# Modulation vectors on VectorE: 512 columns at a time, four blocks a TensorE turn

## The chip, the cores and the metric

The kernel runs on one core of one Trainium2 chip. The metric is the device time of one execution in microseconds (us), the median of several runs. TensorE is called PE, VectorE DVE, ScalarE ACT, GpSimd POOL and SyncE SP, as in the profile. TensorE's clock has two levels, 2.4 GHz and 1.2 GHz; the profile gives the granted share of the higher one.

## The reference, cut to what matters

Two transformer blocks on 512 tokens of width 1024, all in float32: a first block (retention heads, attention, a gated merge, a feed-forward of width 4096) and a second of two layers (with 256 context tokens beside the 512 in the first layer). Each block scales and shifts its activations by vectors that come from a conditioning vector:

```python
def ada_params(cond, w, b):
    m = jax.nn.silu(cond) @ w + b          # cond: [1024], w: [1024, 6144]
    return jnp.split(m, 6, axis=-1)        # shift, scale, gate (twice)

def modulate_2(h, shift, scale):
    return h * (1 + scale) + shift
```

The second block takes two such vectors per layer (one for the tokens, one for the context) from the same weights. In all that is three weight matrices of 1024 x 6144, or 3 x 48 blocks of 128 output columns. The first 16 blocks are needed before the first weight product and are computed ahead of it; this is not touched. The other 128 blocks, numbered a = 0 to 127, are computed beside the rest: a = 0 to 31 with one vector (first block), 32 to 79 and 80 to 127 with two (the layers of the second block).

## The kernel before, in words

Every large weight product is done in units of 256 weight columns (`gemm`, L543 to L545). A unit with 8 row tiles of 128 (KT = 8) has 48 matmuls of 512 columns, one with 4 row tiles has 24; with context, half as many again of 256 columns. The float32 weights are split in two parts: SP loads `raw`, ACT copies it to `w_hi` (`hi`, L1066 or L1074), DVE subtracts to get `w_lo` (`lo`, L1600), and PE multiplies hi by hi, hi by lo and lo by hi. Buffers alternate between two units: `hi(n+1)` waits until unit n-1 is done, so `hi` and `lo` of the next unit must fit beside unit n on PE. PE's unit n+2 also waits until ACT has taken the results of unit n out of PSUM (`psum_free`). In the second half of a feed-forward ACT takes them to `y_t` (L1342) and DVE adds them to X (`residual`, L1859); in the first half ACT takes `r_t` (L1325), DVE squares it (L1843), ACT and DVE split it (L1847).

The order of each engine's instructions is written out by hand, with loops over heads and over feed-forward blocks; the tables at the top of the file say after which unit a piece of modulation work is placed. Before the change one block a of 128 columns goes this way:

- POOL loads all 8 row tiles of the block into `ada_raw` (L2204), multiplies by the conditioning vector with a broadcast (L2213), and adds the 8 row tiles in three halvings (L2215, L2217, L2219), once per vector; then it raises `ada_sum`. Before block a it waits until PE has done step a-2.
- PE sums over the partitions: one product with a column of ones for each vector (`ada_mm_step`, L671), placed after a unit. It waits for `ada_sum` and for `ada_evac`, that is until DVE has taken the result of the block before. Each product appears as two records in the profile. The result lies in one PSUM column per vector.
- DVE takes it out and adds the bias (`ada_out` L1643, `ada_outs` L1653), and raises `ada_evac`.

In each of the four retention heads there are eight such steps (L664 to L730). The order on DVE there is: `lo(n+1)`; for heads 1 to 3 `z_f32(h-1)`, a reciprocal and eight scaled products that end the head before (L1659, L1662, L1666); a take; `lo(n+2)`; `z_low`; a take; and on. On PE it is: `gemm(n)`, a step, `gemm(n+1)`, a step, the four short units of the z product (L543 with z_hi), and on. `rotate` (L1680 to L1686) stands on DVE between the `lo` of the second and of the third of these short units.

Of the kernel before, what the change touches and what calls it, by code (L numbers as in the profile page):

```python
# [58 lines left out]
ADA = {"gate_a": [1, 1, 0, 1], "ret_out": [0, 1, 0, 0], "att0": [1, 1, 1, 1, 0, 1, 1, 1, 0], "att1": [1, 1, 1, 1, 0, 1, 1, 1, 0],  # L59
       "gate_b": [1, 1, 0, 1], "att_out": [0, 1, 0, 0], "w_o": [1, 1, 1, 1],  # L60
       "ff_head": [1, 1], "ff_body": [1, 0, 0, 1, 0, 1, 0, 1, 0, 1, 0, 1], "ff_tail": [1, 0, 0, 0, 1, 0, 0, 0, 0, 0],
       "w_in_0": [1] * 9, "w_out_0": [1] * 4, "ff_head_0": [1, 1], "ff_body_0": [1, 1, 0, 1, 1, 1, 1, 1, 0, 1, 1, 1],
       "ff_tail_0": [1, 0, 1, 0, 1, 0, 0, 0, 0, 0]}
# [37 lines left out]
def ada_starts():  # L101

    start, a = {}, 32
    for name in ADA:
        start[name] = a
        a += sum(ADA[name]) * (3 if "body" in name else 1)
    return start, a
# [18 lines left out]
def build(nc, d, out):  # L126
    FU, RESULTS, WITH_CTX = unit_plan()
    ADA0, ADA_END = ada_starts()
    assert ADA0["w_in_0"] == 80 and ADA_END == 128, (ADA0, ADA_END)
# [7 lines left out]

    def ada_first(name, k, i=0):
        return ADA0[name] + sum(ADA[name][:k]) + (i * sum(ADA[name]) if "body" in name else 0)
# [6 lines left out]
    with ctx:  # L146
# [4 lines left out]
        def sem(name):  # L151
# [3 lines left out]
        o = 16512  # L155
# [29 lines left out]
        ada_raw = [at(f"ada_raw{i}", [P, KT, P], F32, o + 4096 * i) for i in range(2)]  # L185
        ada_prod = at("ada_prod", [P, KT, P], F32, o + 8192)
        ada_acc = at("ada_acc", [P, 2, 2, P], F32, o + 12288)
        o += 14336
# [31 lines left out]
                at("ada0_2", [P, KT, 512], F32, F1 + 40960), at("ada0_3", [P, KT, 512], F32, 16512 + 32768)]  # L220
# [320 lines left out]
        def _(pe):  # L541
# [121 lines left out]
            ada_par = [0]  # L663

            def ada_mm_step(a, vecs=1, bank_=C1):

                pe.wait_ge(ada_sum, a + 1)
                if not (isinstance(a, int) and a == 0):
                    pe.wait_ge(ada_evac, a)
# [5 lines left out]
            def ada_steps(name, k, i=0):  # L675

                for j in range(ADA[name][k]):
                    ada_mm_step(ada_first(name, k, i) + j, 2, X1 if name.endswith("_0") else C1)

            def ret_head(h, n, with_out, first=False):  # L680
                gemm(n, 0, hs_hi, hs_lo, ready=(hs_ready, lambda k: k + 1) if first else None)
                ada_mm_step(8 * h)
                gemm(n + 1, 1, hs_hi, hs_lo)
                ada_mm_step(8 * h + 1)
# [19 lines left out]
                ada_mm_step(8 * h + 2)  # L704
                ada_mm_step(8 * h + 3)
# [12 lines left out]
                ada_mm_step(8 * h + 4)  # L718
                ada_mm_step(8 * h + 5)
# [11 lines left out]
                ada_mm_step(8 * h + 7)  # L731
# [4 lines left out]
            for j in range(4):  # L736
                gemm(FU["gate_a"] + j, j % 2, hs_hi, hs_lo)
                ada_steps("gate_a", j)
            for j in range(4):
                if j == 0:  # L740
                    pe.wait_ge(zlo_done, 4)
                gemm(FU["ret_out"] + j, j % 2, z_hi, z_lo, 4)
                ada_steps("ret_out", j)
# [33 lines left out]
            for p_ in range(2):  # L777
                n = FU["att0"] + 9 * p_
                for hh in range(2):
                    for g in range(GROUPS):  # L780
                        gemm(n + 6 * hh + g, (n + 6 * hh + g) % 2, hs_hi, hs_lo)
                        ada_steps(f"att{p_}", 6 * hh + g)
                    if hh == 0:
                        for g in range(GROUPS):
                            gemm(n + 3 + g, (n + 3 + g) % 2, hs_hi, hs_lo, tokens=tile_tok)
                            ada_steps(f"att{p_}", 3 + g)
# [14 lines left out]
            for j in range(4):  # L801
                gemm(FU["gate_b"] + j, (FU["gate_b"] + j) % 2, hs_hi, hs_lo)
                ada_steps("gate_b", j)
            for j in range(4):
# [3 lines left out]
                ada_steps("att_out", j)  # L808
            for j in range(4):
                gemm(FU["w_o"] + j, j % 2, m_hi, m_lo, ready=(mlo_done, lambda k: k + 1) if j == 0 else None)  # L810
                ada_steps("w_o", j)
            norm_sums()

            def feed_forward(n0, sec, nr, mf, ready, cready, suffix):
# [4 lines left out]
                def ada_(name, k, i=0):  # L819
                    if suffix is not None:  # L820
                        ada_steps(name + suffix, k, i)
# [68 lines left out]
            for l in range(2):  # L890
# [7 lines left out]
                for u in range(9):  # L898
# [5 lines left out]
                    if wc:  # L904
                        ada_steps("w_in_0", u)
                pe.wait_ge(psum_free, R(n + 9))
                if wc:
                    pe.wait_ge(ada_evac, ada_first("w_out_0", 0))
# [121 lines left out]
                for j in range(4):  # L1030
                    gemm(n + 9 + j, (n + 9 + j) % 2, hs_hi, hs_lo, cact=(hc_hi, hc_lo) if wc else None)
                    if wc:
                        ada_steps("w_out_0", j)
# [521 lines left out]
        def _(dve):  # L1555
# [84 lines left out]
            def ada_out(a):  # L1640

                dve.wait_ge(ada_mm, a + 1)
                dve.tensor_tensor(mod1[:, bass.ds(16 + a, 1)], C1[:, 0:1], vec1[:, bass.ds(24 + a, 1)],  # L1643
                                  ALU.add).then_inc(ada_evac, 1)

            def ada_outs(name, k, i=0):

                l, bank_ = (1, X1) if name.endswith("_0") else (0, C1)
                for j in range(ADA[name][k]):
                    a = ada_first(name, k, i) + j  # L1650
                    dve.wait_ge(ada_mm, a + 1)
                    j_ = a - (80 if l else 32)
                    dve.tensor_scalar(mod2[l][:, :, bass.ds(j_, 1)], bank_[:, 0:2].rearrange("p (v o) -> p v o", o=1),  # L1653
                                      vec2[:, l, bass.ds(j_, 1)], None, ALU.add).then_inc(ada_evac, 1)
# [40 lines left out]
            def ret_head(h, n, with_out):  # L1695
# [3 lines left out]
                ada_out(8 * h)  # L1699
# [3 lines left out]
                ada_out(8 * h + 1)  # L1703
# [630 lines left out]
```

## Time and profile before

| | |
|---|---|
| median of three runs | 3314.33 us (3310.28 to 3318.7) |
| the profiled execution | 3322.18 us, its span 3320.5 us |
| mean granted clock of TensorE | 0.955 |
| busy: PE, DVE, ACT, POOL | 3055.3, 1714.8, 1181.4, 1347.8 us |
| stages, from PE's timeline | start to about 92 us, heads to 554, gates and attention to 1040, feed-forward of the first block to 1431, second block's first layer to about 2549, second layer to 3290 |

Times in rows are microseconds from the start of the span. A busy PE means that its stream of matmuls goes on; two matmuls of 512 columns start 0.23 us apart though each is shown as 0.39 us long, since they overlap. What costs time is where the start of a matmul comes later than that. POOL is busy in the table's sense only with its arithmetic; issuing a transfer takes it under a microsecond.

### The profile page before, as it was taken

How to read it: one execution, taken by the hardware profiler on the slowest of the kernel's cores; microseconds unless marked ns; L12 is line 12 of the kernel's file. 1: busy time of each engine (PE TensorE's matmuls, PEld its weight loads, DVE VectorE, ACT ScalarE, POOL GpSimd, SP SyncE). 2: the span in 40 equal slices, each digit the busy share in tenths (PEclk: the TensorE clock that was granted, in tenths of full speed). 3: DMA queues.
4: the chain of work that ended last, by engine and by line, in shares of the span. 5: the costliest groups of instructions: out<-in, count | busy, mean ns of one | idle time of the engine just before them, and what ended most of it. 6: DMA issues, size and time to landing. Idle time of an engine off the chain costs nothing.

```text
span 3320.5 us, 42497 instructions
## 1 busy us (share of the span) xinstructions
PE 3055.3 (92%) x16079; PEld 2564.3 (77%) x16079; DVE 1714.8 (52%) x1792; ACT 1181.4 (36%) x1683; POOL 1347.8 (41%) x1044
## 2 busy tenths in 40 slices
PE   5799999999988999989988989999999988989998
PEld 3677777788776788859787768787887968868886
DVE  4563454533355776651286357555554338444444
ACT  2232333223333333342255343232324326433443
POOL 2455346774556777716500147777770000000000
PEclk7899999999999999999997899999999999999999
DMA  8333332453433344322310112222322230013331
GB/s 268 115 107 100 113 118 89 138 151 101 125 100 104 102 127 133 120 65 89 99 36 1 32 58 89 90 89 83 96 83 77 69 94 3 26 57 102 95 101 64
DMA packets 260466, 307.50 MB, mean 93 GB/s; under 512 B 23467, under 2 KB 231739, under 8 KB 260316
## 3 DMA queue, kind: packets, MB, share of 16 engines
q1 hardware_dynamic: 234716, 224.43, 21.7%
q0 software_dynamic: 19456, 72.00, 7.2%
q10 hardware_dynamic: 6144, 8.91, 0.9%
q8 instruction: 112, 1.84, 0.2%
q14 instruction: 38, 0.31, 0.0%
HBM read 294.05 MB, written 11.27 MB: 92 GB/s over the span
## 4 chain that ended last, share of the span: by engine, by line
POOLq 32%; PE 32%; issue 26%; DVE 5%; DVEq 1%; POOL 1%; SPq 1%; ACT 1%; DMA 0%; ACTq 0%
POOLq L2214 12%; POOLq L2216 9%; PE psum L543 9%; PE psum L544 8%; PE psum L545 8%; POOLq L2218 6%; POOLq L2222 4%; POOL ada_raw L2204 1%; PE psum L877 1%; PE psum L715 1%; DVE w_lo L1600 1%; PE psum L887 1%; SPq L434 1%; PE psum L621 1%; PE psum L700 1%
## 5 line engine op out<-in xcount | busy, mean ns | idle before, releaser
L2213 POOL TENSOR_TENSOR ada_prod<-ada_raw,csil 128x1024 f32<-128x1024 f32 x224 | 458.6, 2047 | 728.7 <-PE psum L671 708.4
L543 PE MATMUL psum<-hs_hi,w_hi 128*128 128x512 f32 x1632 | 655.3, 402 | 61.3 <-DVE hs_lo L1592 35.5
L1600 DVE TENSOR_TENSOR w_lo<-raw,w_hi 128x2048 fp32r<-128x2048 f32 (+1 forms) x244 | 535.7, 2196 | 292.5 <-ACT w_hi L1066 226.1
L545 PE MATMUL psum<-hs_lo,w_hi 128*128 128x512 f32 x1632 | 644.4, 395 | 0.0
L544 PE MATMUL psum<-hs_hi,w_lo 128*128 128x512 f32 x1632 | 644.3, 395 | 0.0
L2215 POOL TENSOR_TENSOR ada_prod<-ada_prod 128x512 f32<-128x512 f32 x224 | 365.0, 1630 | 193.4 <-issue 179.6
L543 PEld LDWEIGHTS psum<-hs_hi,w_hi 128*128 128x128 f32 x1632 | 312.5, 192 | 132.1 <-issue 44.1
L545 PEld LDWEIGHTS psum<-hs_lo,w_hi 128*128 128x128 f32 x1632 | 311.8, 191 | 67.8
L544 PEld LDWEIGHTS psum<-hs_hi,w_lo 128*128 128x128 f32 x1632 | 313.0, 192 | 63.2
L543 PE MATMUL psum<-mid_hi,w_hi 128*128 128x512 f32 x768 | 303.4, 395 | 4.0 <-DVE w_lo L1600 3.9
L545 PE MATMUL psum<-mid_lo,w_hi 128*128 128x512 f32 x768 | 300.1, 391 | 0.0
L544 PE MATMUL psum<-mid_hi,w_lo 128*128 128x512 f32 x768 | 299.6, 390 | 0.0
L1859 DVE TENSOR_TENSOR X<-X,y_t 128x512 f32<-128x512 f32 x208 | 197.1, 957 | 171.9 <-ACT y_t L1342 171.9
L1843 DVE TENSOR_TENSOR r_t<-r_t 128x512 f32<-128x512 f32 x112 | 119.3, 1067 | 314.5 <-ACT r_t L1325 314.4
L1342 ACT ACTIVATE y_t<-psum,mod 128x512 f32<-128x512 f32 x208 | 143.1, 690 | 338.3 <-PE psum L545 320.0
L2217 POOL TENSOR_TENSOR ada_prod<-ada_prod 128x256 f32<-128x256 f32 x224 | 247.0, 1103 | 31.9
L1325 ACT ACTIVATE r_t<-psum 128x512 f32<-128x512 f32 x112 | 67.0, 599 | 455.8 <-PE psum L545 455.7
L543 PE MATMUL psum<-w_hi,hs_hi 128*128 128x256 f32 x704 | 200.3, 285 | 0.0
L544 PE MATMUL psum<-w_hi,hs_lo 128*128 128x256 f32 x704 | 199.2, 283 | 0.0
L545 PE MATMUL psum<-w_lo,hs_hi 128*128 128x256 f32 x704 | 199.2, 283 | 0.0
L1074 ACT CAST w_hi<-raw 128x2048 fp32r<-128x2048 f32 (+1 forms) x138 | 190.6, 1381 | 0.0
L1066 ACT CAST w_hi<-raw 128x2048 fp32r<-128x2048 f32 (+1 forms) x106 | 174.3, 1645 | 14.8 <-issue 8.9
(332 smaller groups left out, 5668.0 us busy)
## 6 DMA issues: line engine op xcount, KB each, us to landing
raw<-in_w_in SPq DMA_DIRECT2D x56, 1024.0 KB, 5.1
ada_raw<-in_ada_w POOLq DMA_DIRECT2D x96, 512.0 KB, 4.7
raw<-in_w_ff SPq DMA_DIRECT2D x48, 1024.0 KB, 5.5
raw<-in_w_ff SPq DMA_DIRECT2D x96, 512.0 KB, 3.5
ada_raw<-in_w_ada POOLq DMA_DIRECT2D x32, 512.0 KB, 4.7
raw<-in_w_in SPq DMA_DIRECT2D x24, 512.0 KB, 5.2
ada<-in_w_ada SPq DMA_DIRECT2D x4, 2048.0 KB, 24.1
raw<-in_w_ret_out SPq DMA_DIRECT2D x16, 512.0 KB, 3.4
```

The costliest lines, as they stand in the source:

```text
L543: pe.matmul(dst, lhi, rhi, start=start, stop=False)
L544: pe.matmul(dst, llo, rhi, start=False, stop=False)
L545: return pe.matmul(dst, lhi, rlo, start=False, stop=stop)
L1074: act.copy(w_hi[n0_ % 2][:, 0:kt], raw[n0_ % 2][:, 0:kt]).then_inc(hi_done, 1)
L1600: dve.tensor_tensor(w_lo[par][:, 0:kt], raw[par][:, 0:kt], w_hi[par][:, 0:kt].bitcast(F32), ALU.subtract).then_inc(lo_done, 1)
L1859: dve.tensor_tensor(X[:, q, :], X[:, q, :], y_t[r_][:], ALU.add).then_inc(y_free, 1)
L2213: pool.tensor_tensor(ada_prod[:], ada_raw[par][:], bass.AP(c_.tensor, c_.offset, [*c_.ap, [0, P]]), ALU.mult)
L2214: pool.drain()
L2215: pool.tensor_tensor(ada_prod[:, 0:4], ada_prod[:, 0:4], ada_prod[:, 4:8], ALU.add)
L2216: pool.drain()
L2217: pool.tensor_tensor(ada_prod[:, 0:2], ada_prod[:, 0:2], ada_prod[:, 2:4], ALU.add)
L2218: pool.drain()
```

## The change

PE and DVE are given other modulation work, and POOL only issues the loads. The 128 blocks become 32 groups g of 512 columns (four blocks). A load brings two row tiles of 512 columns (the same 512 KB as before), so a group has four loads; the work on one load is a slot s = 0 to 127.

- DVE does a slot with one operation per row tile and vector: the first of a group multiplies (`tensor_scalar`), the others multiply and add to `ada_acc` (`scalar_tensor_tensor`), all on 128 x 512, with a drain between the row tiles. That is two operations for a slot of the first 32 and four for the others. It raises `ada_sum` after each slot.
- PE does a turn per group: it waits for `ada_sum` >= 4g+4 and `ada_evac` >= g, and does four blocks for each vector one behind the other.
- DVE takes four columns per vector at once (`ada_take1`, `ada_take2`).
- POOL waits before load s until slot s-2 is done.
- The tables say where slots, turns and takes stand. In a head slots 0 and 1 stand behind `lo(n+4)`, 2 to 4 behind `lo(n+5)`, 5 to 7 behind `lo(n+6)`.
- `ada_prod` goes, the SBUF offsets move, and the scratch for POOL's transfers is halved (`dynamic_dma_scratch_size=8192`).

```diff
+ADA_SLOTS = {"gate_a": [1] * 4, "att0": [1] * 8 + [0], "att1": [1] * 8 + [0], "gate_b": [1] * 4,
+             "ff_body": [1, 1, 1, 0, 1, 0] * 2, "w_in_0": [2] * 8 + [0], "w_out_0": [1] * 4,
+             "ff_body_0": [1, 1, 1, 0, 1, 0] * 2, "ff_tail_0": [1] * 4 + [0] * 6}
+
+ADA_TURNS = {"gate_a": {0: 7}, "ret_out": {0: 8}, "att0": {4: 9}, "att1": {0: 10, 4: 11}, "gate_b": {0: 12}, "att_out": {0: 13},
+             "ff_body": {5: 14, 11: 15}, "w_in_0": {2: 20, 4: 21, 6: 22, 8: 23}, "ff_head_0": {1: 24},
+             "ff_body_0": {5: 25, 11: 26}, "ff_tail_0": {4: 31}}
+
+ADA_TAKES = {"gate_a": {0: 6, 2: 7}, "ret_out": {2: 8}, "att0": {6: 9}, "att1": {2: 10, 6: 11}, "gate_b": {2: 12},
+             "ff_body": {0: 13, 6: 14}, "ff_tail": {0: 19}, "w_in_0": {3: 20, 5: 21, 7: 22},
+             "ff_body_0": {0: 24, 6: 25}, "ff_tail_0": {0: 30, 5: 31}}
...
+            def ada_turn(g, par, vecs=1, bank_=C1):
+
+                pe.wait_ge(ada_sum, 4 * g + 4)
+                if not (isinstance(g, int) and g == 0):
+                    pe.wait_ge(ada_evac, g)
                 for v in range(vecs):
-                    mm = pe.matmul(bank_[:, v:v + 1], ada_acc[:, ada_par[0], v, :], ones_c[:, 0:1], start=True, stop=True)
-                ada_par[0] ^= 1
+                    for b in range(4):
+                        mm = pe.matmul(bank_[:, 4 * v + b:4 * v + b + 1], ada_acc[par][:, v, b * P:(b + 1) * P], ones_c[:, 0:1],
+                                       start=True, stop=True)
                 mm.then_inc(ada_mm, 1)
...
             def ret_head(h, n, with_out, first=False):
                 gemm(n, 0, hs_hi, hs_lo, ready=(hs_ready, lambda k: k + 1) if first else None)
-                ada_mm_step(8 * h)
+                if with_out:
+                    ada_turn(2 * h - 1, 1)
                 gemm(n + 1, 1, hs_hi, hs_lo)
-                ada_mm_step(8 * h + 1)
...
-                ada_mm_step(8 * h + 6)
                 gemm(n + 5, 1, hs_hi, hs_lo)
+                ada_turn(2 * h, 0)
                 pe.wait_ge(gsq_done, h + 1)
...
+            def ada_slot(s, i=None, two=True):
+
+                par, kp = s % 2, s % 4
+                acc = ada_acc[s // 4 % 2]
+                if kp:
+                    dve.drain()
+                dve.wait_ge(ada_in[par], 16 * (s // 2 + 1) if i is None else 64 * i + 16 * (s // 2 + 1))
+                for kk in range(2):
+                    k = 2 * kp + kk
+                    if kk:
+                        dve.drain()
+                    for v in range(2 if two else 1):
+                        c_ = csil2[:, v, k:k + 1] if two else csil[:, k:k + 1]
+                        if k == 0:
+                            last = dve.tensor_scalar(acc[:, v, :], ada_raw[par][:, kk, :], c_, None, ALU.mult)
+                        else:
+                            last = dve.scalar_tensor_tensor(out=acc[:, v, :], in0=ada_raw[par][:, kk, :], scalar=c_,
+                                                            in1=acc[:, v, :], op0=ALU.mult, op1=ALU.add)
+                last.then_inc(ada_sum, 1)
...
                 lo(n + 1, 1)
                 if with_out:
                     z_f32(h - 1)
-                ada_out(8 * h)
+                    ada_take1(2 * h - 2)
                 lo(n + 2, 0, 4 if with_out else KT)
                 if with_out:
                     z_low(h - 1)
-                ada_out(8 * h + 1)
+                    ada_take1(2 * h - 1)
...
-                ada_out(8 * h + 2)
-                ada_out(8 * h + 3)
                 lo(n + 4, 0)
-                ada_out(8 * h + 4)
-                ada_out(8 * h + 5)
+                for s in range(2):
+                    ada_slot(s, h, False)
                 lo(n + 5, 1)
+                for s in range(2, 5):
+                    ada_slot(s, h, False)
                 dve.wait_ge(mu_done, h + 1)
                 dve.tensor_tensor(ro[:], ro[:], bc(X1[:], 4), ALU.subtract).then_inc(d_sub, 1)
-                ada_out(8 * h + 6)
                 lo(n + 6, 0)
-                ada_out(8 * h + 7)
+                for s in range(5, 8):
+                    ada_slot(s, h, False)
...
+            def load_ada(w, c, kp, par):
+                pool.dma_start(ada_raw[par][:], w[:, 2 * kp:2 * kp + 2, bass.ds(c, 512)]).then_inc(ada_in[par], 16)
```

In the units of a feed-forward and of the attention a slot stands behind `lo` of the next unit and ahead of `residual` or of the squares.

## Rows read from the trace of the kernel before

**Rows 1.** The page's busy table, whole span.
```profile
PE 3055.3 (92%) x16079; PEld 2564.3 (77%) x16079; DVE 1714.8 (52%) x1792; ACT 1181.4 (36%) x1683; POOL 1347.8 (41%) x1044
```
**Rows 2.** PE's timeline (start, duration in us): steps between products of weights.
```profile
565.60 0.50 PE L671 MATMUL psum<-ones_c,ada_acc 128*128 128x1 f32 x4
565.96 0.49 PE L543 MATMUL psum<-hs_hi,w_hi 128*128 128x512 f32 x1
...
207.03 0.28 PE L671 MATMUL psum<-ones_c,ada_acc 128*128 128x1 f32 x2
207.17 0.48 PE L543 MATMUL psum<-hs_hi,w_hi 128*128 128x512 f32 x1
```
**Rows 3.** PE's timeline: stops in the feed-forward with context.
```profile
2140.94 0.28 PE L545 MATMUL psum<-midc_lo,w_hi 128*128 128x256 f32 x1
2146.30 1.01 PE L671 MATMUL psum<-ones_c,ada_acc 128*128 128x1 f32 x4 [5.08 <-POOL ada_acc L2219]
2150.19 0.79 PE L543 MATMUL psum<-hs_hi,w_hi 128*128 128x512 f32 x1 [2.88 <-issue]
...
2443.97 1.01 PE L671 MATMUL psum<-ones_c,ada_acc 128*128 128x1 f32 x4 [5.16 <-POOL ada_acc L2219]
```
**Rows 4.** PE's timeline: stops that DVE ends, the idle time in brackets.
```profile
144.60 0.35 PE L671 MATMUL psum<-ones_c,ada_acc 128*128 128x1 f32 x2 [0.76 <-DVE mod L1643]
...
220.72 0.49 PE L543 MATMUL psum<-z_hi,w_hi 128*128 128x512 f32 x1 [2.29 <-DVE z_lo L1672]
...
235.67 0.49 PE L543 MATMUL psum<-z_hi,w_hi 128*128 128x512 f32 x1 [2.15 <-DVE w_lo L1600]
...
581.46 0.80 PE L543 MATMUL psum<-hs_hi,w_hi 128*128 128x512 f32 x1 [3.97 <-DVE w_lo L1600]
...
991.32 0.79 PE L543 MATMUL psum<-m_hi,w_hi 128*128 128x512 f32 x1 [5.53 <-DVE w_lo L1600]
```
**Rows 5.** Groups by line (busy us, mean ns): 1075 to 1430 us, then 2960 to 3290.
```profile
L1859 DVE TENSOR_TENSOR X<-X,y_t 128x512 f32<-128x512 f32 x62 | 76.5, 1251 | 27.9 <-ACT y_t L1342 27.9
...
L1859 DVE TENSOR_TENSOR X<-X,y_t 128x512 f32<-128x512 f32 x63 | 43.4, 692 | 62.2 <-ACT y_t L1342 62.2
L1600 DVE TENSOR_TENSOR w_lo<-raw,w_hi 128x1024 fp32r<-128x1024 f32 x32 | 39.2, 1225 | 8.0 <-ACT w_hi L1074 6.0 <-ACT w_hi L1066 2.0
...
L1074 ACT CAST w_hi<-raw 128x1024 fp32r<-128x1024 f32 x24 | 25.0, 1043 | 0.0
```
**Rows 6.** Stretches: length, then busy PE, PEld, DVE, ACT, POOL; granted clock.
```profile
2150.00:2153.00 3.00, 2.81 (x7) 2.24 (x8) 2.06 (x1) 0.00 (x0) 1.15 (x1) 0.50 0.25 85
221.00:226.00 5.00, 5.00 (x16) 3.91 (x16) 5.00 (x3) 0.56 (x1) 4.48 (x4) 0.66 0.33 101
1075.00:1430.00 355.00, 349.21 (x1564) 287.74 (x1563) 248.29 (x194) 136.53 (x172) 265.10 (x198) 1.00 0.40 121
```
**Rows 7.** PE's timeline: first and last product of two feed-forwards.
```profile
1061.43 0.77 PE L543 MATMUL psum<-hs_hi,w_hi 128*128 128x512 f32 x1 [13.35 <-DVE hs_lo L1592]
...
1431.44 0.39 PE L545 MATMUL psum<-mid_lo,w_hi 128*128 128x512 f32 x1
...
2939.69 0.77 PE L543 MATMUL psum<-hs_hi,w_hi 128*128 128x512 f32 x1 [8.74 <-DVE hs_lo L1592]
...
3290.50 0.39 PE L545 MATMUL psum<-mid_lo,w_hi 128*128 128x512 f32 x1
```
**Rows 8.** Timelines of POOL and DVE at 92 us.
```profile
91.99 0.92 POOL L2204 DMA_DIRECT2D ada_raw<-in_w_ada  x1 [0.57 <-issue]
...
92.06 0.75 DVE L1588 SCALAR_TENSOR_TENSOR n_t<-X,scale,n_rstd 128x512 f32<-128x512 f32 x1
```
**Rows 9.** DVE's timeline: the chain between two heads.
```profile
198.62 3.29 DVE L1600 TENSOR_TENSOR w_lo<-raw,w_hi 128x2048 fp32r<-128x2048 f32 x1 [2.24 <-ACT w_hi L1074]
...
208.28 5.86 DVE L1666 SCALAR_TENSOR_TENSOR ro<-ro,vec,sgate 128x512 f32<-128x512 f32 x4 [0.17 <-issue]
```
**Rows 10.** The page's DMA issues: count, KB each, us from issue to landing.
```profile
ada_raw<-in_w_ada POOLq DMA_DIRECT2D x32, 512.0 KB, 4.7
```

More of the change, by code:

```diff
@@ L101, in ada_starts @@
 def ada_starts():
[L103 to L107, printed above, removed]
+    first, s = {}, 32
+    for name, slots in ADA_SLOTS.items():
+        first[name] = s
+        s += sum(slots) * (3 if "body" in name else 1)
+    assert first["w_in_0"] == 80 and s == 128, (first, s)
+    return first
 class Item:
@@ L184, in build @@
         o += 6144
[L185 to L188, printed above, removed]
+        ada_raw = [at(f"ada_raw{i}", [P, 2, 512], F32, o + 4096 * i) for i in range(2)]
+        ada_acc = [at(f"ada_acc{i}", [P, 2, 512], F32, o + 8192 + 4096 * i) for i in range(2)]
+        o += 16384
         H0 = o
@@ new lines, in ada_take1, with ada_take2 @@
+            def ada_take1(g):
+                dve.wait_ge(ada_mm, g + 1)
+                dve.tensor_tensor(mod1[:, bass.ds(16 + 4 * g, 4)], C1[:, 0:4], vec1[:, bass.ds(24 + 4 * g, 4)],
+                                  ALU.add).then_inc(ada_evac, 1)
+            def ada_take2(g, l):
+                dve.wait_ge(ada_mm, g + 1)
+                c0 = 4 * g - (80 if l else 32)
+                for v in range(2):
+                    last = dve.tensor_tensor(mod2[l][:, v, bass.ds(c0, 4)], (X1 if l else C1)[:, 4 * v:4 * v + 4],
+                                             vec2[:, l, bass.ds(c0, 4)], ALU.add)
+                last.then_inc(ada_evac, 1)
@@ L1656, in z_f32, with ada_part @@
+            def ada_part(name, k, i=None):
+                if k in ADA_TAKES.get(name, {}):
+                    g = ADA_TAKES[name][k]
+                    if g < 8:
+                        ada_take1(g)
+                    else:
+                        ada_take2(g if i is None else g + 2 * i, 1 if g >= 20 else 0)
+                if name in ADA_SLOTS:
+                    for j in range(ADA_SLOTS[name][k]):
+                        ada_slot(ADA0[name] + sum(ADA_SLOTS[name][:k]) + j, i)
             def z_f32(h):
@@ L1821, in _ @@
                         merge_lo(q - 1)
-                ada_outs("att_out", j)
             merge_lo(7)
@@ L1904, in tail @@
                     lx(n0 + 39 + j)
-                    if j:
-                        after("ff_tail", j - 1)
+                    part("ff_tail", j)
                 hidden(7, n0 + 38, tail, 1, sec, nr, mf)
-                after("ff_tail", 1)
                 second(n0 + 40, lambda j: lx(n0 + 41 + j), "ff_tail", 2)
@@ L2249, in _, with loads @@
-            for par in range(2):
-                chunk(126 + par, par, 1024, (0, 1))
+            def load_ada(w, c, kp, par):
+                pool.dma_start(ada_raw[par][:], w[:, 2 * kp:2 * kp + 2, bass.ds(c, 512)]).then_inc(ada_in[par], 16)
+            def loads(w, c0, s0, groups):
+                with pool.Fori(0, groups) as i:
+                    for kp in range(4):
+                        pool.wait_ge(ada_sum, s0 + 4 * i + kp - 1)
+                        load_ada(w, c0 + 512 * i, kp, kp % 2)
@@ L2253, in constants @@
+            for kp in range(2):
+                load_ada(wada, 2048, kp, kp)
+            for kp in range(2, 4):
+                pool.wait_ge(ada_sum, kp - 1)
+                load_ada(wada, 2048, kp, kp % 2)
+            loads(wada, 2560, 4, 7)
+            for l in range(2):
+                loads(wada2[l], 0, 32 + 48 * l, 12)
 def constants():
```

139 lines of the change are left out of this document (33 added, 106 removed).

## The prediction

> **What bounds the kernel now.** I read the busy table first, then PE's timeline for what stands between its matmuls, then what DVE and POOL did there. PE is busy for 92% of the span [rows 1], so in most stages time is PE's stream of weight products, and only what interrupts it costs. POOL's long idle time and the large share of the chain that goes through it cost nothing by themselves: most of it is POOL waiting for PE. What the reader is to see is (a) a modulation step inside the stream: four records of L671 cost 0.36 us from their first start to the next product (565.60 to 565.96), two cost 0.14 [rows 2], so a record in a row costs (0.36-0.14)/2 = 0.11 us and the first hides behind the product before it; (b) places where PE stands still for POOL [rows 3]; (c) places where it stands still for DVE [rows 4], which is slow there because POOL computes beside it: the same X<-X,y_t operation takes 1251 ns in the first block's feed-forward and 692 ns in the last one, where POOL does nothing [rows 5].
>
> **Part 1: POOL computes nothing any more, PE no longer waits for it.** In the feed-forward with context PE reaches a step at the end of a loop turn before POOL has summed: from 2140.94 to 2150.19, 9.25 us where a product's pitch and a step need 0.12+0.36, so 8.8 lost [rows 3]. Then the granted clock is 0.50 for 3 us [rows 6], the lower of its two levels: half of 3.2 us, 1.6 lost. The loop does this three times; the last, at 2443.97, goes on at once and costs 5.16 of idle time, 0.6 for records at the lower clock, and 1.6 behind them. Sum 10.4+10.4+7.4 = 28 us. Afterwards the slots there are one per unit and a group's last slot lies a unit before its turn, in units of 8 to 16 us: nothing replaces the wait. Term: -28.
>
> **Part 2: DVE at its own speed.** The first block's feed-forward runs from 1061.43 to 1431.44, 370.0 us; the last one, same products, no POOL, from 2939.69 to 3290.50, 350.8 [rows 7]. Of the 19.2 us, 22 steps of 0.36 are 7.9; the other 11.3 are waits for a slowed DVE: -11.3. The norm ahead of it makes PE wait 13.35 us, the same norm without POOL 8.74 [rows 7]: -4.6. At 991.32 PE waited 5.53 us for w_lo behind eight slowed merge operations per unit [rows 4]; at 0.69 each that DVE work fits PE's 5.5 us units, and the lower clock after it goes too (1.6): -7.1. Smaller waits of the same kind stand ahead of the first product, in att_out, ret_out and the first attention unit: between 0 and 12, I take -7.
>
> **Part 3: the slots that DVE takes over.** 32 slots of two operations and 96 of four on 128x512, 448 in all. Such an operation (two inputs in SBUF, one a scalar pointer) takes 0.75 us with POOL not computing; it did so right beside a POOL transfer issue too [rows 8]. The upper bound is the 1.25 us of the slowed X row [rows 5]. A four-operation slot is 4x0.67 (starts overlap by 0.07) plus drains, 2.9 us; all slots are some 310 us of DVE time, about what it gains from the end of contention, so DVE stays near 1700 us, half the span [rows 1]. Behind a slot wait the residual or squares of the same unit. Worked through for a 5.45 us unit of the feed-forward: ACT's last evacuation ends 0.9 after PE starts the unit, its hi takes 1.05 and lo 1.2 [rows 5], so lo ends 3.2 after the start, the slot 6.1, the previous product's residual was done earlier and this one's ends 7.5; the next lo starts at 7.5 and ends 8.7, PE wants it at 10.9. Cover 2 us, 0.8 to 1.2 in the first of the four units; units with a KT=8 lo have no slot. Cost 0; +2 for places I can't see.
>
> **Part 4: turns of four blocks.** The count of records is unchanged (448), but only the first of a turn hides. A two-vector turn has 16 records: 0.03+15x0.11 = 1.70 us for 4x0.36 = 1.44, over 24 turns +6.2. A one-vector turn has 8: 0.81; per head the eight steps cost 4x0.14+2x0.36 = 1.28 and become 1.62, in all +1.3. Term: +7.5. The waits of PE for DVE's take between two steps placed together go (0.76 us at 144.60 [rows 4], a second of about 0.5 per head): 4x1.25 = -5.
>
> **Part 5: the heads, where a new wait stands.** Before, PE waits 2.29 us for z_lo at 220.72 [rows 4], and the clock is 0.66 for 5 us after it [rows 6], 1.7 more; three times, and once 3.97+1.7 for the w_lo behind z_f32 at 581.46. DVE's chain is lo, reciprocal, eight products, where the last four take 5.86 us and lo 3.29 [rows 9]; at 4x0.67 and 2.25 it ends 4.1 us earlier, and both waits go: -12.0 and -5.7. But the order of the takes changes. PE's turn 2h-1 stands right behind gemm(n) and waits for ada_evac >= 2h-1, that is for take 2h-2, and DVE does that take only behind lo(n+1) and z_f32(h-1). Before, the step at this place waited only for a take done in the head before. The chain ends at about 214.14 [rows 9] less 4.1 plus 0.6 (the turn ahead of the variance products shifts PE and all that follows) = 210.7; PE is there at 207.0+0.6 [rows 2]. It stands 3.2 us, does eight records at the lower clock (0.21 each, as it does after every such stop: 1.01 for four at 2146.30 [rows 3]), 0.8 more, and loses 1.7 behind: 5.7, three times, and at gate_a (take 6 behind z_f32(3)) 2.7+2.4: +22.2. Queued behind PE's wait are gemm(n+1) and everything after; nobody covers it. The wait for w_lo behind rotate (2.15 at 235.67 [rows 4]) stays: it hangs on the end of gemm(n+1) and 12 rotate operations; with no z stop before it it shows 0.6 longer, +2.
> The three slots in a row (2 to 4, 5 to 7) make DVE wait for a load that is issued when the first of them ends. From issue to landing 4.7 us [rows 10]: slot 7 ends about 198, hi(n+1) is due at 199. Hidden with 1 us of cover.
>
> **Sum.** -28-11.3-4.6-7.1-7-5-12-5.7 = -80.7; +2+7.5+22.2+2 = +33.7; together -47. The profiled execution took 3322.2 us (span 3320.5) and becomes 3275; it lies 7.9 above the median 3314.3, so the median becomes **3267**.
>
> **A rule of the skill against it.** The issue beside a DVE operation took 0.92 us and the operation 0.75 [rows 8]. The Trainium skill ("SBUF — State Buffer", Who interferes with whom) says that tensor_scalar can enter a mode that takes the port pair shared with GpSimd, which then can't write its transfers' descriptors. By the rows each load lands 4.7 us after its issue; by the rule the first operation of each group would hold up issues that fall on it by its own 0.5 us or so. No row shows a tensor_scalar of DVE on this. Late loads, whatever makes them late, are the third rival.
>
> **Rivals.**
> (1) The take-behind-z wait isn't there or is covered (the eight z products and lo run faster than I take, or ACT's hi comes earlier): all of part 5's +22 goes. 3245. For: 3.2 us is a difference of sums of ten operations. Against: the order in the code is plain, and the reciprocal in it isn't slowed by POOL, so it gains nothing. Decides if take 2h-2 ends within 7 us of lo(n+1)'s start; it needs about 11.
> (2) Forecast.
> (3) Slots or their loads come late: 1 to 3 us more of DVE in the heads (three slots in a row, landing 7 instead of 4.7 us) and in the 5.45 us units, whose cover is 0.8 to 1.2. At 1 us in each of some 25 places: 3290.
> (4) Slower than before: the contention isn't POOL's arithmetic but its presence (transfers issued, its reads), and DVE goes on at 1.25 us. The first feed-forward has DVE busy 248 of 355 us [rows 6]; 96 slot operations at 1.25 add 120, 368 > 355, DVE becomes the bound there (+13 and no gain), part 2 is void, the take wait is 3.2+4.1+2.5 (x4, +39), turns +7.5, part 1 still -28, the z waits stay. 3314+32 = about 3345. It decides from 1.1 us per operation in that stage. Against: 0.75 beside an issue, and 692 ns without POOL [rows 5, 8].
> (5) PE is bound elsewhere, so that nothing of part 2 shows: only 28 and 22 cancel: 3310, no change.
>
> **Numbers.** Forecast 0.55, (1) 0.18, (3) 0.17, (4) 0.05, (5) 0.05. Range 3243 to 3298: holds (1) and (3), leaves out (4) and (5). Faster or slower is told from 0.3%, 10 us, as a measurement can. Faster 0.90, same 0.05, slower 0.05.
>
> **What would show it.** Right: L1859 at about 690 ns in every stage and DVE near 1700 us in sum; no PE wait for a sum near the three loop ends; the first feed-forward 361 us (350.8+6x1.70); at each of heads 1 to 3 an L671-like turn that starts about 3 us late, released by DVE's take into mod; 16 records at a 0.11 pitch. Wrong: no such wait (rival 1), waits for w_lo or ada_raw spread over the feed-forward (3), or L1859 above 1 us (4).

## The result, and the profile after

| | before | after |
|---|---|---|
| median of the runs, us | 3316.51 (3310.28 to 3320.64, 4 runs) | 3256.42 (3254.37 to 3258.83, 4 runs) |
| profiled execution, us | 3322.18 | 3258.83 |
| span, us | 3320.5 | 3257.2 |
| granted TensorE clock, mean | 0.955 | 0.963 |

The changed kernel takes 0.9821 of the time of the one before, with a 95% interval of 0.9802 to 0.9839: 60 us less by the medians, 63.3 between the two profiled executions. 3267 was forecast, in 3243 to 3298: the likeliest case, 11 us too high by the medians and 16 by the profiled executions (3275 was forecast there).

The page's busy table of the changed kernel answers to [rows 1]:
```profile
PE 3036.1 (93%) x16079; PEld 2553.1 (78%) x16079; DVE 1685.3 (52%) x2168; ACT 1179.8 (36%) x1683; POOL 102.5 (3%) x148
```
POOL's 1348 us of work are 103, and DVE, which took over 448 operations, is busy 30 us less. Its groups by line over the whole span (count | busy us, mean ns | idle time before and what ended it) say why:
```profile
L1597 DVE TENSOR_TENSOR w_lo<-raw,w_hi 128x2048 fp32r<-128x2048 f32 x128 | 293.3, 2292 | 467.9 <-ACT w_hi L1063 354.0 <-ACT w_hi L1071 113.7
L1653 DVE SCALAR_TENSOR_TENSOR ada_acc<-ada_raw,csil,ada_acc 128x512 f32<-128x512 f32 x392 | 279.8, 749 | 32.4 <-DMA ada_raw<-in_w_ada 13.0 <-issue 3.0
L1885 DVE TENSOR_TENSOR X<-X,y_t 128x512 f32<-128x512 f32 x208 | 141.1, 690 | 168.6 <-ACT y_t L1339 168.6
L1651 DVE TENSOR_SCALAR ada_acc<-ada_raw,csil 128x512 f32<-128x512 f32 x56 | 24.9, 481 | 12.9 <-DMA ada_raw<-in_w_ada 12.8
```
The mean of X<-X is now 690 ns over all stages ([rows 5] had 1251 in one and 692 in another), and a slot operation takes the 0.75 us of [rows 8]. The slots hold DVE up for their loads by 26 us in the whole span, all of it in the 32 loads of the first block; but for the four turns below, no turn on PE waits.

PE's timeline between the first two heads, then DVE's:
```profile
200.55 0.39 PE L547 MATMUL psum<-hs_lo,w_hi 128*128 128x512 f32 x1
204.22 1.84 PE L672 MATMUL psum<-ones_c,ada_acc 128*128 128x1 f32 x8 [3.29 <-DVE mod L1660]
205.92 0.78 PE L545 MATMUL psum<-hs_hi,w_hi 128*128 128x512 f32 x1
```
```profile
194.81 3.35 DVE L1687 RECIPROCAL gn_rstd<-gn_std 128x512 f32<-128x512 f32 x1
198.36 2.74 DVE L1690 SCALAR_TENSOR_TENSOR ro<-ro,vec,gn_rstd 128x512 f32<-128x512 f32 x4 [0.20 <-issue]
201.27 2.74 DVE L1694 SCALAR_TENSOR_TENSOR ro<-ro,vec,sgate 128x512 f32<-128x512 f32 x4 [0.17 <-issue]
203.92 0.15 DVE L1660 TENSOR_TENSOR mod<-psum,vec 128x4 f32 x1
```
This is the new wait of part 5 (3.29 is the idle time in brackets; where the text counts a stop from the time at which the next start was due, it is 0.14 to 0.16 longer, 3.45 here): the turn's records wait for the take of the turn before, and that take stands behind the z products. The stops of 2.29 and 3.97 us for z_lo and w_lo [rows 4] are gone. In stretches of the changed kernel (length; busy PE, PEld, DVE, ACT, POOL; then the granted clock), the clock is at the lower of its two levels until about 210:
```profile
204.00:207.00 3.00, 2.78 (x11) 2.61 (x12) 0.16 (x3) 2.85 (x2) 0.00 (x0) 0.50 0.00 0
207.00:210.00 3.00, 3.00 (x9) 2.33 (x8) 3.00 (x2) 0.00 (x0) 0.00 (x0) 0.50 0.13 26
210.00:213.00 3.00, 3.00 (x14) 2.46 (x13) 0.42 (x2) 0.00 (x0) 0.00 (x0) 0.95 0.47 155
```
The first feed-forward, which answers to [rows 7], by its first and last product:
```profile
1033.62 0.77 PE L545 MATMUL psum<-hs_hi,w_hi 128*128 128x512 f32 x1 [8.73 <-DVE hs_lo L1589]
...
1395.62 0.39 PE L547 MATMUL psum<-mid_lo,w_hi 128*128 128x512 f32 x1
```
362.0 us in place of 370.0, with the norm's stop ahead of it at 8.73 in place of 13.35. In the feed-forward with context no wait for POOL is left, but at two of the three loop ends PE still stands still, here from 2100.69. These are pieces of the chain of waits in order of time (start, us, what):
```profile
2099.01 1.68 PE psum L672 x16
2100.69 3.17 issue
2103.86 0.79 PE psum L545
```
"Issue" is time in which PE waited for nothing that the profile shows. The same 2.88 us stood in [rows 3], behind the wait for POOL. In PE's sequencer a compare-and-branch lasts 4.86 us there (3.52 before), and 0.24 at the loop ends of the feed-forward without context rows.

With each weight product of one trace laid beside the same product of the other, the 62.5 us come from (stretches by the times of before; the forecast has the terms of the prediction, part 4's 0.26 for each two-vector turn in the stretch where the turn stands):

| stretch of before, us | forecast | measured |
|---|---|---|
| 0 to 127, and 606 to 960 (start, gates, attention) | -5.4 | -11.3 |
| 127 to 606, heads and first gate | +2.8 | +0.1 |
| 960 to 1028, att_out and w_o | -7.1 | -11.9 |
| 1028 to 1061, norm | -4.6 | -4.7 |
| 1061 to 1432, first feed-forward | -9.7 | -8.0 |
| 1432 to 1985, the second block's first attention | +1.3 | -4.2 |
| 1985 to 2460, feed-forward with context | -26.2 | -22.2 |
| the rest, and +2 for slots | +2 | -0.3 |

### The profile page after: what moved, and what is told of

It reads as the page before. It is cut to its first block, busy times and chain, and to the rows that moved or that the text cites. A ratio compares the mean times of both kernels' runs of the same rounds, so it can differ in the third digit from the quotient of the medians.

```text
span 3257.2 us, 40990 instructions
## 1 busy us (share of the span) xinstructions
PE 3036.1 (93%) x16079; PEld 2553.1 (78%) x16079; DVE 1685.3 (52%) x2168; ACT 1179.8 (36%) x1683; POOL 102.5 (3%) x148
## 4 chain that ended last, share of the span: by engine, by line
PE 84%; DVE 6%; DVEq 3%; ACT 2%; issue 2%; SPq 1%; DMA 1%; ACTq 0%
PE psum L545 24%; PE psum L546 24%; PE psum L547 24%; PE psum L874 3%; PE psum L623 2%; PE psum L884 2%; PE psum L672 2%; PE psum L715 1%; DVE w_lo L1597 1%; DVE n_t L1585 1%; SPq L436 1%; PE psum L771 1%; DVEq L1584 1%; PE psum L702 1%; ACT w_hi L1063 0%
## 5 line engine op out<-in xcount | busy, mean ns | idle before, releaser
L1597 DVE TENSOR_TENSOR w_lo<-raw,w_hi 128x2048 fp32r<-128x2048 f32 (+1 forms) x244 | 435.4, 1785 | 549.1 <-ACT w_hi L1063 382.1
L1653 DVE SCALAR_TENSOR_TENSOR ada_acc<-ada_raw,csil,ada_acc 128x512 f32<-128x512 f32 x392 | 279.8, 749 | 32.4 <-DMA ada_raw<-in_w_ada 13.0
L1869 DVE TENSOR_TENSOR r_t<-r_t 128x512 f32<-128x512 f32 x112 | 77.4, 692 | 327.9 <-ACT r_t L1322 327.7
L1885 DVE TENSOR_TENSOR X<-X,y_t 128x512 f32<-128x512 f32 x208 | 141.1, 690 | 168.6 <-ACT y_t L1339 168.6
L547 PEld LDWEIGHTS psum<-mid_lo,w_hi 128*128 128x128 f32 x768 | 144.3, 188 | 30.0
L545 PEld LDWEIGHTS psum<-mid_hi,w_hi 128*128 128x128 f32 x768 | 144.3, 188 | 29.1
```

Of the source, the lines that this page charges most:

```text
L545: pe.matmul(dst, lhi, rhi, start=start, stop=False)
L547: return pe.matmul(dst, lhi, rlo, start=False, stop=stop)
L1597: dve.tensor_tensor(w_lo[par][:, 0:kt], raw[par][:, 0:kt], w_hi[par][:, 0:kt].bitcast(F32), ALU.subtract).then_inc(lo_done, 1)
L1653: last = dve.scalar_tensor_tensor(out=acc[:, v, :], in0=ada_raw[par][:, kk, :], scalar=c_, in1=acc[:, v, :], op0=ALU.mult, op1=ALU.add)
L1869: dve.tensor_tensor(r_t[r_][:], r_t[r_][:], r_t[r_][:], ALU.mult).then_inc(midf_done, 1)
L1885: dve.tensor_tensor(X[:, q, :], X[:, q, :], y_t[r_][:], ALU.add).then_inc(y_free, 1)
```

## The experiments

Each was timed in turns with the kernel before, the first four below in one session, the next (a turn one unit earlier) and the last (slots doubled) in another, and the four between them in a third. Between sessions the ratios to before and the traces are what can be compared. "After" means the changed kernel.

**The changed kernel again.** 

> The changed kernel once more, as the yardstick of the three beside it. 0.982 of the kernel before, about 3256 us. PE's four stops behind the take into mod (3.45, 3.44, 3.45, 3.23 us) and the two at the end of the context loop (3.31, 2.85 us) should be there again.

Measured: 3254.73 us (5 runs), 0.9812 of before (0.9796 to 0.9827). The four stops behind the take are the same (3.45, 3.45, 3.45, 3.23 us); the two at the loop ends are 2.75 and 2.63 here, where after had 3.31 and 2.85. From 127 to 606 this trace of the same kernel is 3 us shorter than after's, so a difference of that size in the heads shows nothing.

**The take ahead of the z products.**
```diff
                 lo(n + 1, 1)
                 if with_out:
-                    z_f32(h - 1)
                     ada_take1(2 * h - 2)
+                    z_f32(h - 1)
...
                 if j == 0:
+                    ada_take1(6)
                     z_f32(3)
```
Take 6 goes out of the table `ADA_TAKES` for this.

> One move on DVE: the take of turn 2h-2 is done ahead of the z products of head h-1, not behind them (and take 6 ahead of z_f32(3) in gate_a). Forecast's theory, the take behind z is a wait of PE's own: the four turns with their stops go from 5.15, 5.14, 5.01 and 4.93 us to about 0.8 each, 17 us less than the changed kernel, 3239 us. PE then reaches the products with z_lo 4.3 us earlier, at about 211.9 in the profile's time where z_lo ends at 210.4, so no wait takes the place. Rival, the stop only stands in front of another: PE waits for z_lo or w_lo instead and 3 us or less per head come back, 3250 us or more. A third: with no stop of 3.4 us the wait of 2.57 us for w_lo behind the rotation (229.6) grows; I expect it unchanged, since it hangs on the end of the product before it.

Measured: 3230.47 us, 0.9746 (0.973 to 0.9763), 24.3 less than after in the same session. PE's timeline at the same place:
```profile
199.87 0.39 PE L547 MATMUL psum<-hs_lo,w_hi 128*128 128x512 f32 x1
200.10 0.94 PE L672 MATMUL psum<-ones_c,ada_acc 128*128 128x1 f32 x8
200.91 0.49 PE L545 MATMUL psum<-hs_hi,w_hi 128*128 128x512 f32 x1
```
The stops are gone in all four places and no other took their place; the one for w_lo behind the rotation stayed at 2.57 us. Of 6.3 us per place 4.3 are the stop and its slower records; the other 2.0 (1.8 to 2.5 against after's trace) are the products behind it at the lower clock, which this expectation left out and the prediction had (1.7). The +22.2 of part 5 is shown: 24 by the medians, 24 against after's trace from 127 to 606 and 21 against that of the changed kernel again.

**The context loop written out.**
```diff
-                with pe.Fori(0, 3) as i:
+                def body(i):
                     for q in range(2):
...
+                if nr == 3:
+                    for i in range(3):
+                        body(i)
+                else:
+                    with pe.Fori(0, 3) as i:
+                        body(i)
```


> One change on PE: the three turns of the context feed-forward's loop are written out, so its taken branches are gone (a compare-and-branch there lasts 4.86 and 4.40 us in PE's sequencer, 0.24 and 0.21 in the loop without context rows). Theory A, the stops of 3.31 and 2.85 us at the two loop-back ends are the branch itself (the loop's first instructions fetched again), 0.36 behind each: 6 to 7 us less than the changed kernel, 3250 us. Theory B, they are the price of fetching that code in whatever form: written out it is as long, the stops spread out or move, 3256 us. Theory C, the straight code is fetched worse than the loop: slower than 3260 us.

Measured: 3250.15 us, 0.9795 (0.9778 to 0.9812), 4.6 less than after, and the intervals overlap. The trace decides. The same loop end:
```profile
2102.24 0.28 PE L547 MATMUL psum<-midc_lo,w_hi 128*128 128x256 f32 x1
2102.36 1.84 PE L672 MATMUL psum<-ones_c,ada_acc 128*128 128x1 f32 x16
2104.07 0.47 PE L545 MATMUL psum<-hs_hi,w_hi 128*128 128x512 f32 x1
```
1.71 us from the records to the next product, where it was 5.01, and that product at full clock. The stage is 10.8 us shorter than after's, 5.4 for each of the two loop ends (8.9 against the changed kernel again), with nothing spread out elsewhere in it. The stop is the taken branch of this loop (A); B and C are out. What the branch waits for isn't shown. Of the gain 4.2 us were lost again in the attention ahead of it, on which the edit doesn't bear (below).

**Both.** 

> Both edits together, since they lie 1500 us apart: the sum of the two gains, 23 to 24 us less than the changed kernel, 3233 us, if both theories hold; if they share a cause, less than the sum.

Measured: 3219.81 us, 0.9705 (0.9692 to 0.9718), 34.9 less than after: 24.6 by the trace in the heads, 10.8 at the two loop ends. It is above the 23 to 24 expected because the clock loss behind the stops was left out there, and above the sum of the two measured gains (28.8) in part because the single run of the loop lost 4.2 us in the attention, this one 0.8.

**A turn one unit earlier.** The second turn of the loop at index 10, its slots at 6 to 9:
```diff
-             "ff_body_0": [1, 1, 1, 0, 1, 0] * 2, "ff_tail_0": [1] * 4 + [0] * 6}
+             "ff_body_0": [1, 1, 1, 0, 1, 0, 1, 1, 1, 1, 0, 0], "ff_tail_0": [1] * 4 + [0] * 6}
-              "ff_body_0": {5: 25, 11: 26}, "ff_tail_0": {4: 31}}
+              "ff_body_0": {5: 25, 10: 26}, "ff_tail_0": {4: 31}}
```


> The changed kernel with the second turn of the context feed-forward's loop one unit earlier (index 10, not 11), its slots at indices 6 to 9: no record stands between the loop's last product and its taken branch. If the stops of 3.31 and 2.85 us there are the branch, they stay (the queue in front of it then holds 128x256 products of 0.12 us instead of records of 0.11): within 2 us of the changed kernel. If the row of records in front of the branch makes them, they go: 6 us less, 3250 us.

Measured: 3260.39 us (4 runs), 0.9817 (0.9796 to 0.9838): no change. Stops of 2.62 and 2.51 us stay with no record near:
```profile
2106.62 0.49 PE L545 MATMUL psum<-hs_hi,w_hi 128*128 128x512 f32 x1 [2.46 <-issue]
```

**The kernel before with POOL's arithmetic cut down.** One 128x128 addition per vector is left of four operations; POOL is busy 254 us in place of 1348.
```diff
-                    pool.tensor_tensor(ada_prod[:], ada_raw[par][:], bass.AP(...), ALU.mult)
...
-                    last = pool.tensor_tensor(ada_acc[:, par, v, :], ada_prod[:, 0], ada_prod[:, 1], ALU.add)
+                    last = pool.tensor_tensor(ada_acc[:, par, v, :], ada_raw[par][:, 0], ada_raw[par][:, 1], ALU.add)
```


> The kernel before, with GpSimd's product with the condition and two of its three halvings left out: it adds the first two row tiles of the raw block, one 128x128 operation for each vector, so the modulation vectors are not those of the reference. Steps, takes, loads and DVE's work are those of before. It isolates parts 1 and 2 (PE's waits for the sum, DVE slowed beside POOL) and the z waits, without slots, turns of four or the new wait. By my terms: -28-11.3-4.6-7.1-7 and -12-5.7 for the z waits, less about 6 for the branch at the loop ends that now shows: 3247 us, X<-X at about 700 ns in all stages. Rival, DVE's slowness comes from the issue of transfers or costs PE nothing: only the 22 us of part 1 go, 3294 us.

Measured: 3239.26 us (4 runs), 0.9765 (0.9749 to 0.978), 77 less than before. By line, its DVE:
```profile
L1859 DVE TENSOR_TENSOR X<-X,y_t 128x512 f32<-128x512 f32 x208 | 143.3, 691 | 251.3 <-ACT y_t L1342 251.3
```
So POOL's silence (parts 1 and 2 and the z waits of part 5) is the whole gain; the rest of the change costs, 17 us by the medians and 16 to 19 by the ratios. The z waits are in it: no stop for z_lo is left, and from 127 to 606 this kernel gains 16.2, where -12 and -5.7 were forecast. Product beside product, it and after gain alike in most stages behind the heads (606 to 960 -7.5 and -7.4, att_out and w_o -11.7 and -11.9, first feed-forward -8.1 and -8.0). Up to 606 they part by 15.1 us in after's disfavour, which is the new wait less the waits between two steps that the turns removed; from 1432 to 1985 they part by 8.0 the other way (what stays open, below). This trace is of an execution 12 us above the median. The context loop gives -24.7 here. At its ends the branch shows too:
```profile
2095.58 0.49 PE L543 MATMUL psum<-hs_hi,w_hi 128*128 128x512 f32 x1 [2.20 <-issue]
```
22 steps of four records with DVE at full speed take a first feed-forward to 361.9 us, six turns of 16 (eight records more) take it to 362.0: a turn costs what its four steps cost, to about a microsecond in the stage.

**After, with POOL computing again for nobody.** Behind each load of the second and third layers:
```diff
                         load_ada(w, c0 + 512 * i, kp, kp % 2)
+                        if s0 >= 32:
+                            pool.tensor_tensor(p_scr[:], p_scr[:], bass.AP(csil, ...), ALU.mult)
+                            for k in (4, 2, 1):
+                                pool.drain()
+                                pool.tensor_tensor(p_scr[:, 0:k], p_scr[:, 0:k], p_scr[:, k:2 * k], ALU.add)
```


> The changed kernel, and GpSimd does four operations per load (product with the condition and three halvings, on a scratch tile of its own that nobody reads) behind each of the 96 loads of the second and third layers' vectors, from about 585 us on. Nobody waits for them; a load's issue can be up to 5.4 us later. It puts back DVE's contention alone. If contention is the price: X<-X and slot operations go back to 1.2 us and more where POOL works, the first feed-forward takes 15 us more, the norm before it 4, att_out and w_o 7, the rest some 8: about 35 us more than the changed kernel, 3290 us. Rival, PE is bound elsewhere and DVE has the room: within 5 us of 3256.

Measured: 3275.76 us (4 runs), 0.9889 (0.987 to 0.9909), about 20 more than after. By the traces 18.3 of it lie in the first feed-forward, where 15 were expected, though POOL computes less there than in before (132 us against 265); PE stops five times for w_lo. Another 4.2 lie from 554 to 606: the reciprocal and z products beside a computing POOL end later, and the fourth stop for the take grows from 3.07 us of idle time to 7.07. From 1052 to 1415 us, DVE's groups, then the first of the stops:
```profile
L1654 DVE SCALAR_TENSOR_TENSOR ada_acc<-ada_raw,csil,ada_acc 128x512 f32<-128x512 f32 x84 | 65.4, 819 | 3.9 <-issue 1.0
L1598 DVE TENSOR_TENSOR w_lo<-raw,w_hi 128x1024 fp32r<-128x1024 f32 x32 | 60.3, 1883 | 3.8 <-ACT w_hi L1064 2.0 <-ACT w_hi L1072 1.8
L1886 DVE TENSOR_TENSOR X<-X,y_t 128x512 f32<-128x512 f32 x62 | 58.1, 964 | 18.4 <-ACT y_t L1340 18.4
```
```profile
1094.05 0.49 PE L546 MATMUL psum<-mid_hi,w_hi 128*128 128x512 f32 x1 [2.29 <-DVE w_lo L1598]
```
The rest of the expectation failed: in the norm, att_out and w_o DVE has no slot, so POOL had no load and hence no arithmetic there. From 606 to 960 POOL computed and this kernel still gained the same 7.3 as after; the stops that went there stood at 617 to 645 of before, where this kernel has no POOL arithmetic either. Where it does bear, the slowed DVE alone makes PE wait, with nobody waiting for POOL: the mechanism of part 2, and it falls on w_lo.

**Records one by one.** On the kernel with both edits, PE's matmuls of a turn between weight products:
```diff
                 pe.matmul(dst, lhi, rhi, start=start, stop=False)
+                if records:
+                    records.pop(0)()
                 pe.matmul(dst, llo, rhi, start=False, stop=False)
```


> The kernel with the early takes and the unrolled context loop (3219.8 us), and the records of a turn no longer stand in a row behind a unit: each stands alone between two weight products of the unit's second half (where the unit has no token form; in three or four places they stay in a row). The claim behind part 4 is that only the first record of a row hides (0.03 us) and each further one costs 0.11. If so a record that stands alone costs 0.03, a turn of 16 costs 0.5 in place of 1.70: about 20 turns x 1.2 + 8 x 0.5 = 28 us less, 3192 us. Rival, every record costs its weight load of 0.11 wherever it stands: no change, 3220 us. Third, a record between products also makes the next product wait for its weights: 0.14 and more each, 3230 us or above.

Measured: 3220.81 us, 0.9713 (0.97 to 0.9727): no change against 3219.81 (0.9705), the rival. One matmul is two records in the trace, and what they cost is seen only with the product behind them:
```profile
1073.41 0.39 PE L545 MATMUL psum<-mid_hi,w_hi 128*128 128x512 f32 x1
1073.64 0.28 PE L688 MATMUL psum<-ones_c,ada_acc 128*128 128x1 f32 x2
1073.78 0.48 PE L548 MATMUL psum<-mid_hi,w_lo 128*128 128x512 f32 x1
1074.09 0.28 PE L688 MATMUL psum<-ones_c,ada_acc 128*128 128x1 f32 x2
1074.23 0.47 PE L551 MATMUL psum<-mid_lo,w_hi 128*128 128x512 f32 x1
```
The record starts "hidden", 0.23 behind the product before it, and the next product 0.14 later; but from there to the next start it is 0.31, not 0.23. From product to product, 1073.78 to 1074.23, it is 0.45: 0.22 for two records, 0.11 each, as in a row. Nothing hides.

**w_lo between the two halves of the rotation.** On the kernel with both edits:
```diff
-                    rotate(h, n)
+                    rotate(h, n, lambda: lo(n + 4, 0, 4))      # called behind the half t == 0
                     for j in range(4):
-                        if j:
+                        if j > 1:
```


> The kernel with the early takes and the unrolled context loop (3219.8 us), and DVE does the w_lo of unit n+4 between the two halves of the rotation, not behind the rotation and two sums: PE's stop of 2.57 us for it at three places (222.6, 336.3, 451.5) should go, 7.7 us less and up to 3 more where the granted clock fell after it: 3210 us. Rival, hi of that unit comes no earlier, or the rotation that ends 1.2 us later makes the score products wait: within 3 us of 3220.

Measured: 3214.93 us (3210.16 to 3219.94, 5 runs), 0.9697 (0.9682 to 0.9711): the lowest median of the study, 5 us under its base. The intervals overlap (the base has 0.9692 to 0.9718), and the traces decide: 9.8 us less in the heads, where nothing else differs. w_lo is done at 221.5, and PE starts on it at 223.89 without a stop:
```profile
220.30 1.23 DVE L1604 TENSOR_TENSOR w_lo<-raw,w_hi 128x1024 fp32r<-128x1024 f32 x1 [0.52 <-ACT w_hi L1078]
```
A new stop of 0.23 us stands at 229.72, for the w_lo of the unit behind, which now comes after the rotation's second half and four additions. Base and edit were not timed in the same session, so the size is known to a few us only.

**Slots doubled.**
```diff
-                if kp:
+                if kp or s >= 32:
                     dve.drain()
...
+                        if s >= 32:
+                            dve.scalar_tensor_tensor(out=d_scr[v][:], in0=ada_raw[par][:, kk, :], scalar=c_,
+                                                     in1=ada_raw[par][:, kk, :], op0=ALU.mult, op1=ALU.add)
```


> The changed kernel, and in the 96 slots of the second and third layers' vectors DVE does each of the four operations twice, the second time on the same inputs into a scratch tile that nobody reads: 384 operations of 0.75 us (a 0.68 pitch) more, 2.7 us per slot, DVE about 1950 us. It measures the cover behind the zero of part 3. My working gave 2 us of cover in the 5.45 us units and 0.8 to 1.2 in the first of the four: then the first feed-forward's 24 slots each make PE wait, 2 us in a quarter of them and 0.7 in the others, some 25 us with the lower clock behind, the 10.9 us units none: 3280 us. Rival, the cover was much larger than worked out (DVE is idle half the time): within 5 us of 3256. Other rival, there was hardly any, each doubled slot shows in full: above 3310 us.

Measured: 3262.76 us (4 runs), 0.9827 (0.9809 to 0.9845), with DVE at 1935.7 us. The medians give 2 us more than the kernel with the earlier turn in the same session, and 6 to 8 more than after in others; the traces say it better: the first feed-forward takes 10.9 us more than after's, where 25 were expected, and this trace happens to be 6.6 shorter in the attention of what stays open. In the first feed-forward PE stops six times, once in 47 us, for w_lo:
```profile
1092.78 0.49 PE L546 MATMUL psum<-mid_hi,w_hi 128*128 128x512 f32 x1 [1.54 <-DVE w_lo L1598]
```
The stop stands behind the slot of the first 5.45 us unit: the cover there is 2.7-1.7 = 1.0, in the 0.8 to 1.2 of the prediction. The other three slots of each six units (one in a 5.45 us unit, two in 10.9 us units) took 2.7 us more of DVE and no stop followed, so their cover is at least that (I had 2). Part 3's zero is right, with 1 us to spare in the tightest unit.

## Why the prediction was right, and where not

The forecast and its range held, and the places of the large gains and of the new wait came as worked out. That it came within 11 us is in part luck: by the table the two feed-forwards gained 5.7 us less than forecast and the other stretches 21 more, 5.5 of it in a stretch whose gain has no known cause.

**Part 1 (-28; measured -24.7 with POOL nearly idle).** The waits for POOL are gone, as said. "Nothing replaces the wait" failed: behind it stood the loop's branch, 3.3 and 2.9 us, and products at the lower clock behind them. The row was there, 2.88 "issue" in [rows 3]; I took it as part of POOL's stop.

**Part 2 (-11.3, -4.6, -7.1, -7).** The mechanism is shown from both sides for the first feed-forward and the z products, by taking the arithmetic away from before and by putting it into after; for the norm, att_out, w_o and the small waits by taking it away only. Norm -4.7 came close. The feed-forward's -11.3 was too large: its 22 steps cost 0.46 each and not 0.36 (part 4), which leaves 9.1 of the 19.2 us for DVE's waits, and -8.0 was measured with the turns in it. att_out and w_o gave 4.8 more: ahead of the 5.53 us stop [rows 4] two of 1.5 and 2.1 us went as well. The small waits were sized too low, -7 for about -11.

**Part 3 (0, +2).** Right: no stop of PE stands behind a slot, and the doubled slots show the cover.

**Part 4 (+7.5, -5).** The waits behind the -5 are gone (only the four turns above wait for a take); they were not priced by themselves. The +7.5 is the term that failed: I read 0.36 us for four records off their first start to the next product's start [rows 2] and gave the first one to the product before it. The 0.10 that was missing stands one product later (565.96 to 566.29 is 0.33 in that trace, where the pitch is 0.23). Four records cost 0.46, 16 cost 1.80, 0.11 each, however grouped: the term is 0. (0.03+15x0.11 is 1.68, not 1.70, which changes nothing.) It did little harm, since the same misreading made part 2 too large by 2.2.

**Part 5 (-12, -5.7, +22.2, +2).** Place, cause and size of the new wait came as worked out: stops of 3.2 to 3.4 us at four places, 24 us in sum. The prediction's fourth stop, 2.7, was 3.2, and 210.7 less 207.6 is 3.1, not the 3.2 that went into the sum. The waits behind -12 and -5.7 are gone, and the stop for w_lo behind the rotation grew from 2.15 to 2.41 us of idle time, 0.3 and not 0.6. Rival 1 is out, and so is rival 3: no load was late for PE. Rival 4 (POOL's presence, not its arithmetic) falls with X<-X at 690 ns beside 128 issues, and rival 5 with the 77 us that POOL's silence gave.

**What stays open.** From 1432 to 1985 the changed kernel gained 4.2 us where the terms gave +1.3. These are stretches with the same work in that attention, of before and of after:
```profile
1800.00:1875.00 75.00, 65.86 (x409) 58.64 (x408) 36.49 (x65) 37.08 (x79) 0.00 (x0) 0.82 0.00 1
```
```profile
1767.00:1838.00 71.00, 61.18 (x414) 53.91 (x413) 37.81 (x68) 36.15 (x78) 0.00 (x0) 0.93 0.01 2
```
POOL does nothing in either; the granted clock differs, 0.82 and 0.93. This stretch of before takes 5.3 to 6.4 us less in after, in the changed kernel again and in five of the edited ones, 0.7 less in the two with only the loop written out or that and the early takes, and nothing less with the earlier turn or with POOL cut down. The kernels with spread records and with the split rotation contain both of these edits, and have the short stretch again. So it isn't the slots, the turns or an edit as such; what decides the clock there was not found, and a trace's total can differ by this much for no reason of the kernel's.

The rule that I weighed against the change was hardly put to the test. POOL's 128 issues took 0.71 us each with the slots on DVE, 0.92 before, and none of them overlapped a tensor_scalar of a slot; the loads landed 4.3 us after their issue in the median and 7.3 at most (4.7 and 7.5 before). The Trainium skill ("SBUF — State Buffer", Who interferes with whom) says that tensor_scalar can block such issues; no run here shows it or speaks against it. The same section says that a DVE operation with two SBUF inputs contends with a GpSimd operation that reads SBUF; by that rule, the trace agrees, 1251 against 690 ns.

## What to carry to other kernels

When an engine leaves the shared work, price first what its neighbour does slower beside it: here 77 us came from POOL falling all but silent, and nothing from fewer, larger turns. An acknowledgement that frees a buffer (here a 0.15 us take) belongs ahead of the long chain on its engine, not behind it: moving it gave 24 us. Measure what a short instruction costs from the product before it to the second product behind it, and look behind every wait that you remove for the one that it covered.

## What the runs showed of the hardware

- Beside a POOL that computed for 265 of 355 us, a DVE operation with two SBUF inputs (X<-X, 128x512) took 1251 ns in the mean; beside one that only issued loads, 690.
- At a taken loop branch of the context feed-forward PE stood idle for 2.2 to 3.2 us before the next product (compare-and-branch 4.0 to 4.9 us in its sequencer, 3.4 and 3.5 in before), and not at all at those of the two feed-forwards without context rows (0.2 us); the last, not taken, takes 0.1 in the sequencer. Written out, the same code ran without a stop.
- A stop of 3.4 us cost 1.8 to 2.5 more behind it, in products at the lower clock (granted 0.50).
- A matmul with one column costs 0.22 us in fp32 at the higher clock, two records of 0.11, in a row or alone.
- tensor_scalar on 128x512 fp32 took 481 ns, the scalar_tensor_tensor with a second input in SBUF 749.
